# Sparse attention of a two-block layer kernel: scores of large blocks issued a block ahead, small blocks normalised ahead of their neighbour's biases, the last query product counted by halves

## The chip, the cores and the metric

The kernel runs on one core of a Trainium2 chip. The metric is the device time of one execution, in microseconds (us), as the median of several runs.

## The reference, cut to what matters

The whole computes two transformer-like blocks on 1024 tokens. The change touches one part of the second block, `dsa_mixer`, a sparse attention with 4 heads of 64 channels that share one key and one value (MQA). An indexer has scored all admissible keys before; each query keeps its 256 best.

```python
limit = (qpos // CHUNK + 1) * CHUNK            # CHUNK = 64
score = jnp.where(key_pos[None, :] < limit[:, None], score, NEG_BIG)
top_val, top_idx = lax.top_k(score, n_sel)     # n_sel = 256
s = jnp.einsum('bqhd,bqkd->bhqk', qb, k_sel) * (SA_DH ** -0.5)
p = jax.nn.softmax(jnp.where(valid[:, None], s, NEG_BIG), axis=-1)
o = jnp.einsum('bhqk,bqkd->bqhd', p, v_sel)
```

## The kernel before

The kernel is a row of stages; each gives every engine its own program, and semaphores order them. Keys are not gathered. Instead, the stage `sparse_attention` computes dense scores of a block of 128 queries against all keys up to the block's end and adds a mask, zero for kept keys and -1e30 for the others. Block b has (b+1)*128 keys. The blocks are taken in the order 0, 7, 1, 6, 2, 5, 3, 4, so that at place n an even n is a small block (1, 2, 3, 4 tiles of 128 keys) and an odd n a large one (8, 7, 6, 5 tiles).

For each block and head, the work goes around the engines:

- PE, `score_heads` (L3281): for two heads at a time, query times key in two parts (high and low part of the keys), to the PSUM tensors ps0 and ps1, each two banks wide. A head's tensor is free again when DVE has added the bias of the head two before.
- DVE, `bias_scores` (L3216 and L3219): scale, mask, maximum, written to `prob`; then the negated maximum.
- ACT, `exps` (L3158): exponential with the sum. These stand in ACT's program between the evictions of the turns.
- DVE, `normalise` (L3224, L3228): reciprocal, then a multiplication in pieces of two or three key tiles.
- PE, `turn` (L3291): four transposes of one key tile, one per head, to ps2; ACT evicts them (L3173).
- PE, `weigh` (L3300): the product with the values, added up in ps3, one step behind the turns.
- ACT copies the output (L3181, rounded), DVE subtracts for its rest (`rest_o`, L3236).

Two blocks share `prob`: even n at its end, odd n at its start, and no two neighbours overlap. PE's program for block n is: scores of heads 0 and 1 of block n+1, then the turns and weighings of block n, with the scores of heads 2 and 3 of block n+1 behind turn 2 (or the last turn), then the last weighing. DVE's is: biases of heads 0 and 1 of n+1, normalise n, biases of heads 2 and 3 of n+1, rest of the output of n-1. Before a block's biases from n=2 on, DVE waits for the first turn of block n-1, in program terms `pt_ready.at(turns.index((n - 1, 0)))`, which counts all turns before that one.

Before the first block, PE makes the query products, one for each pair of heads (`product`, L322, 48 matmuls each), and between them transposes the keys and values. ACT rounds each to `q_parts` (L3152) and DVE subtracts for the rest (L3199). All scores wait for both pairs of heads with all tokens.

The next stage, `merge`, first issues the gate product; its SP queue waits for the last `rest_o`, then loads a residual of 4 MB, and then the weights that follow.

Of the kernel before, what the change touches and what calls it, by code (L numbers as in the profile page):

```python
# [148 lines left out]
def first_then_second_block(nc, a, out):  # L149
    ctx = ExitStack()  # L150
    with ctx:
# [2929 lines left out]
        def sparse_attention(y_hi_t, y_lo_t, score, kv_t, following):  # L3081
# [7 lines left out]
            with ExitStack() as sc:  # L3089
# [21 lines left out]

                def pieces(n):

                    cuts = [*range(0, order[n], 2), order[n] + 1]
                    return list(zip(cuts, cuts[1:])) if order[n] else [(0, 1)]
# [21 lines left out]
                def _(act):  # L3137
# [8 lines left out]
                    for m in range(2):  # L3146
                        if m == 1:
                            round_chunk(act, 2, 0, 2)
                        act.wait_ge(used.sem, after(used, m, 0, 2))
                        for odd in range(2):  # L3150
                            rows = slice(odd * 64, odd * 64 + 64)
                            last = act.activation(q_parts[rows, 2 * m + odd], ps[m][rows], ACT.Copy)  # L3152
                        last.then_inc(evicted.sem, 1)
# [9 lines left out]
                    for n, b in enumerate(order):  # L3163
                        heads = list(range(H)) if n + 1 < TT else []
                        for j in range(b + 1):
                            if j >= 2 and heads:

                                exps(n + 1, heads.pop(0))
                            x = turns.index((n, j))
                            act.wait_ge(pt_ready.sem, pt_ready.at(x + 1))  # L3170

                            act.wait_ge(o_ready.sem, o_ready.at(x - 1))
                            act.activation(prob_t[:, x % 2], ps[2][:, x % 2 * HALF:x % 2 * HALF + HALF], ACT.Copy)\  # L3173
                               .then_inc(pt_evicted.sem, 1)
# [10 lines left out]
                def _(dve):  # L3185
# [8 lines left out]
                    for m in range(2):  # L3194

                        dve.wait_ge(evicted.sem, evicted.at(m + 1))
                        for odd in range(2):
                            rows, other, h = slice(odd * 64, odd * 64 + 64), slice(64 - odd * 64, P - odd * 64), 2 * m + odd
                            last = dve.tensor_tensor(q_parts[other, h], ps[m][rows], q_parts[rows, h].bitcast(F32), ALU.subtract)  # L3199
                        last.then_inc(aux3.sem, 1)  # L3200
                    dve_steps.wait(dve)
# [6 lines left out]
                    def bias_scores(n, heads):  # L3208
                        b = order[n]

                        if n >= 2:
                            dve.wait_ge(pt_ready.sem, pt_ready.at(turns.index((n - 1, 0))))
# [26 lines left out]

                    bias_scores(0, range(H))  # L3240
                    for n in range(TT):
                        if n + 1 < TT:
                            bias_scores(n + 1, (0, 1))
                        normalise(n)
                        if n + 1 < TT:
                            bias_scores(n + 1, (2, 3))
                        if n >= 1:
                            rest_o(n - 1)
                    rest_o(TT - 1)

                @block.tensor
                def _(pe):
# [13 lines left out]
                    product(pe, (1, 0, 2), wide(ps[1])).then_inc(used.sem, 1)  # L3266
# [37 lines left out]
                    score_heads(0, 2)  # L3304
                    for n in range(TT):
                        if n + 1 < TT:
                            score_heads(n + 1, 0)
                        normed = sum(len(pieces(o)) for o in range(n))
                        for j in range(order[n] + 1):
# [7 lines left out]
                            if j == min(2, order[n]) and n + 1 < TT:  # L3317
                                score_heads(n + 1, 2)
                        weigh(n, order[n])
# [3 lines left out]
            for s, n in ((aux, 2), (aux2, 1), (aux3, 2), (transposed, 1), (tr_evicted, 2), (evicted, 2), (scores, TT * H), (biased, TT * H), (mod_ready, TT * H),  # L3323
# [374 lines left out]
```

## Time and profile before

| | |
|---|---|
| median of 3 runs | 3214.3 us (3212.19 to 3214.42) |
| profiled execution, device time | 3210.17 us |
| its span | 3208.4 us |
| PE busy | 3027.8 us, 94% of the span |
| DVE, ACT, POOL busy | 43%, 30%, 32% |
| chain that ended last, by engine | PE 81%, issue 8%, DVE 6%, POOL 2%, ACT 2% |
| sparse attention, first query product to its last weighing | about 2046 to 2188 us into the span |

Over the whole kernel PE is the engine that sets the time, but the share of the span is an average over stages. In the slice of the page that holds this stage PE's busy digit falls from 9 to 8 and 7 and its clock digit to 8. Views of that stretch say more than the page does: the stretches, the waits and the timeline.

### The profile page before, as it was taken

Reading aid. Unit: us, or ns where it says so; the run is one execution under the profiler, and the core shown is the slowest. Engines: PE = TensorE matmul, PEld = TensorE weight load, DVE = VectorE, ACT = ScalarE, POOL = GpSimd, SP = SyncE. Lnnn points to the kernel's source line nnn. Section 1 sums busy time; section 2 is a strip of 40 time slices with the busy share of each in tenths; the row PEclk is TensorE's granted clock in tenths of the full one; section 3 lists DMA queues with packets and bytes.
Section 4 is the critical chain, followed back from the end, with each engine's and each line's share of the span. In section 5 each row is a group of like instructions: output and inputs, shape, how many; then the busy total and the mean of one; then the engine's idle time right before and its main releaser. Section 6 shows DMA issues by size and latency. Waiting matters only on the chain.

```text
span 3208.4 us, 38389 instructions
## 1 busy us (share of the span) xinstructions
PE 3027.8 (94%) x14387; PEld 2425.3 (76%) x14387; DVE 1367.3 (43%) x2172; ACT 952.0 (30%) x1569; POOL 1015.5 (32%) x801
## 2 busy tenths in 40 slices
PE   7999989999998999999989999978978999999998
PEld 3788768888876877888767888746766888888886
DVE  5344430111011035544387999851275232332325
ACT  3345532122222244231354222242333111111113
POOL 2544322233422345122221333302445332332323
PEclk9999999999999999999999999989988999999999
DMA  5211021111212133111111111102121111111111
GB/s 193 54 37 37 11 85 50 53 46 43 66 51 72 49 92 95 38 27 34 27 47 31 46 49 47 39 1 85 57 66 40 51 47 46 46 52 46 46 52 72
DMA packets 261458, 170.53 MB, mean 53 GB/s; under 512 B 23604, under 2 KB 249452, under 8 KB 260205
## 3 DMA queue, kind: packets, MB, share of 16 engines
q1 hardware_dynamic: 259997, 163.93, 17.1%
q10 hardware_dynamic: 1360, 5.24, 0.4%
q8 instruction: 65, 1.06, 0.1%
q14 instruction: 36, 0.29, 0.0%
HBM read 160.69 MB, written 8.45 MB: 53 GB/s over the span
## 4 chain that ended last, share of the span: by engine, by line
PE 81%; issue 8%; DVE 6%; POOL 2%; ACT 2%; DMA 1%; SPq 0%; POOLq 0%; DVEq 0%; ACTq 0%
PE ps L322 64%; PE ps L3539 2%; PE ps L3538 2%; PE ps L3540 2%; PE ps L2404 2%; DVE score L2985 1%; PE ps L971 1%; PE ps L985 1%; POOL w_lo L306 1%; PE ps L543 1%; DVE ssq L1909 1%; DVE h_lo L1899 1%; PE ps L1490 1%; PE ps L1493 1%; DMA rows<-in_norm_ffn_post 0%
## 5 line engine op out<-in xcount | busy, mean ns | idle before, releaser
L322 PE MATMUL ps<-h_hi,w_hi 128*128 128x512 f32 x2864 | 1142.5, 399 | 53.4 <-POOL w_lo L306 22.7
L322 PE MATMUL ps<-h_lo,w_hi 128*128 128x512 f32 x2864 | 1124.7, 393 | 0.0
L322 PE MATMUL ps<-h_hi,w_lo 128*128 128x512 f32 x2864 | 1123.4, 392 | 0.0
L306 POOL TENSOR_TENSOR w_lo<-raw,w_hi 128x512 fp32r<-128x512 f32 (+2 forms) x556 | 658.9, 1206 | 1394.0 <-ACT w_hi L299 1393.8
L322 PEld LDWEIGHTS ps<-h_hi,w_hi 128*128 128x128 f32 x2864 | 543.7, 190 | 177.1 <-issue 39.8
L322 PEld LDWEIGHTS ps<-h_hi,w_lo 128*128 128x128 f32 x2864 | 543.1, 190 | 116.2
L322 PEld LDWEIGHTS ps<-h_lo,w_hi 128*128 128x128 f32 x2864 | 544.1, 190 | 113.2 <-issue 3.1
L299 ACT ACTIVATE w_hi<-raw 128x512 fp32r<-128x512 f32 (+2 forms) x556 | 288.3, 567 | 891.9 <-PE ps L322 683.3
L3488 DVE TENSOR_TENSOR act<-gate,ps 128x1024 f32<-128x1024 f32 x22 | 26.9, 1221 | 446.1 <-PE ps L322 446.1
L3497 DVE TENSOR_TENSOR acc<-acc,ps 128x1024 f32<-128x1024 f32 x160 | 195.3, 1221 | 28.7 <-PE ps L3540 27.9
L1194 DVE TENSOR_TENSOR part<-sig,ps 128x1024 f32<-128x1024 f32 x40 | 48.6, 1215 | 355.6 <-PE ps L322 274.9
L3073 DVE MATCH_REPLACE8 score<-best,score 128x384 f32<-128x384 f32 (+2 forms) x192 | 165.8, 875 | 0.0
L3074 DVE MAX8 best<-score 128x8 f32<-128x384 f32 (+2 forms) x192 | 155.7, 878 | 1.1
L3539 PE MATMUL ps<-w_lo,act_hi 128*128 128x512 f32 x352 | 140.3, 399 | 0.0
L3538 PE MATMUL ps<-w_hi,act_hi 128*128 128x512 f32 x352 | 139.4, 396 | 0.2 <-POOL w_lo L306 0.2
L3540 PE MATMUL ps<-w_hi,act_lo 128*128 128x512 f32 x352 | 138.1, 392 | 0.0
L3428 POOL TENSOR_TENSOR act_lo<-act,act_hi 128x1024 fp32r<-128x1024 f32 x21 | 50.6, 2408 | 187.2 <-ACT act_hi L3459 187.2
L1152 POOL TENSOR_TENSOR acc<-acc,part 128x1024 f32 x40 | 96.9, 2421 | 0.0
L3459 ACT ACTIVATE act_hi<-act 128x1024 fp32r<-128x1024 f32 x22 | 23.3, 1061 | 217.5 <-DVE act L3488 217.5
L3454 ACT ACTIVATE gate<-ps 128x1024 f32<-128x1024 f32 x22 | 22.6, 1027 | 211.2 <-PE ps L322 211.2
L3538 PEld LDWEIGHTS ps<-w_hi,act_hi 128*128 128x128 f32 x352 | 66.1, 188 | 17.1 <-POOL w_lo L306 0.6
L3540 PEld LDWEIGHTS ps<-w_hi,act_lo 128*128 128x128 f32 x352 | 66.1, 188 | 15.7
(423 smaller groups left out, 3589.2 us busy)
## 6 DMA issues: line engine op xcount, KB each, us to landing
raw<-in_w_in SPq DMA_DIRECT2D x88, 512.0 KB, 4.0
raw<-in_w_ffn_gate_up SPq DMA_DIRECT2D x44, 512.0 KB, 3.8
raw<-in_w_out SPq DMA_DIRECT2D x32, 512.0 KB, 3.7
raw<-in_w_gate SPq DMA_DIRECT2D x32, 512.0 KB, 3.6
raw<-in_w_ffn_down SPq DMA_DIRECT2D x22, 512.0 KB, 3.5
w_ada<-in_w_ada SPq DMA_DIRECT2D x8, 1024.0 KB, 7.8
x_tok<-in_x ACTq DMA_DIRECT2D x4, 1024.0 KB, 14.3
residual_gate<-in_w_ada SPq DMA_DIRECT2D x8, 512.0 KB
```

Of the source, the lines that this page charges most:

```text
L299: act.activation(w_hi[:, s, cut], raw[:, s, cut], ACT.Copy).then_inc(rounded.sem, 1)
L306: pool.tensor_tensor(w_lo[:, s, cut], raw[:, s, cut], w_hi[:, s, cut].bitcast(F32), ALU.subtract).then_inc(split.sem, 1)
L322: last = pe.matmul(dst, w[:, chunk[0] % 2, k], x(k), start=(k == ks[0] and n == 0), stop=(k == ks[-1] and n == 2))
L1152: pool.tensor_tensor(to, to, part[:], ALU.add).then_inc(o_evicted.sem, 1)
L2404: last = pe.matmul(bank[:, cut], keys[:, h % 3, cut], q[:, h % 2, cut] if n == 0 else queries[:, h % 3, cut], start=True, stop=True)
L3073: top_steps.done(dve.match_replace(part(b), best[:, j], part(b), TAKEN) if marking else dve.max(best[:, j], part(b)))
L3074: dve.max(best[:, j], part(b)))
L3428: pool.tensor_tensor(act_lo[:, f % 2], act32[:], act_hi[:, f % 2].bitcast(F32), ALU.subtract)\
L3497: dve.tensor_tensor(acc[:, t], acc[:, t], outs[t][:], ALU.add).then_inc(o_evicted.sem, 1)
L3538: pe.matmul(dst[:, c:c + HALF], act_hi[:, f % 2, tokens], w[0], start=first, stop=False)
L3539: pe.matmul(dst[:, c:c + HALF], act_hi[:, f % 2, tokens], w[1], start=False, stop=False)
L3540: last = pe.matmul(dst[:, c:c + HALF], act_lo[:, f % 2, tokens], w[0], start=False, stop=final)
```

## The change

Three things are changed in `sparse_attention`, and nothing outside of it.

1. The second query product is counted by token halves. Its first 24 matmuls (tokens 0 to 511) increment a semaphore of their own. ACT and DVE take this product in two halves of 512 columns instead of one of 1024, and the first block's scores wait for the first half only. The scores of block n=1 wait for the second half. DVE does that last rest behind the first block's biases.
2. Scores of large blocks are issued a block ahead on PE. Heads 0 and 1 of the large block n+2 stand between the last turn and the last weighing of the large block n, and heads 2 and 3 behind the first turn of the small block between them. For n=1, heads 0 and 1 stand ahead of all turns.
3. On DVE the small block n (even) is normalised ahead of all biases of the large block n+1, and the large block n+1 is normalised ahead of the biases of the small block n+2. The biases now wait for the last turn of block n-2, whose place in `prob` they take. On ACT the exponentials of a large block stand from turn 1 of the small block on, where they stood from turn 2 on.

```diff
                     for m in range(2):
                         if m == 1:
                             round_chunk(act, 2, 0, 2)
-                        act.wait_ge(used.sem, after(used, m, 0, 2))
-                        for odd in range(2):
-                            rows = slice(odd * 64, odd * 64 + 64)
-                            last = act.activation(q_parts[rows, 2 * m + odd], ps[m][rows], ACT.Copy)
-                        last.then_inc(evicted.sem, 1)
+                        for cols in Q_CUTS[m]:
+                            if cols.stop < T:
+                                act.wait_ge(sum_ready.sem, sum_ready.at(1))
+                            else:
+                                act.wait_ge(used.sem, after(used, m, 0, 2))
+                            for odd in range(2):
+                                rows = slice(odd * 64, odd * 64 + 64)
+                                last = act.activation(q_parts[rows, 2 * m + odd, cols], ps[m][rows, cols], ACT.Copy)
+                            last.then_inc(evicted.sem, 1)
...
-                            if j >= 2 and heads:
+                            if (j >= 2 if n % 2 else 1 <= j <= 2) and heads:
 
                                 exps(n + 1, heads.pop(0))
...
                         if n >= 2:
-                            dve.wait_ge(pt_ready.sem, pt_ready.at(turns.index((n - 1, 0))))
+                            dve.wait_ge(pt_ready.sem, pt_ready.at(turns.index((n - 2, order[n - 2])) + 1))
...
+                    rest_q(0, 0)
+                    rest_q(1, 0)
                     bias_scores(0, range(H))
-                    for n in range(TT):
-                        if n + 1 < TT:
-                            bias_scores(n + 1, (0, 1))
+                    rest_q(1, 1)
+                    for n in range(0, TT, 2):
                         normalise(n)
-                        if n + 1 < TT:
-                            bias_scores(n + 1, (2, 3))
+                        bias_scores(n + 1, (0, 1))
+                        bias_scores(n + 1, (2, 3))
                         if n >= 1:
                             rest_o(n - 1)
+                        normalise(n + 1)
+                        if n + 2 < TT:
+                            bias_scores(n + 2, (0, 1))
+                        rest_o(n)
+                        if n + 2 < TT:
+                            bias_scores(n + 2, (2, 3))
                     rest_o(TT - 1)
...
-                    product(pe, (1, 0, 2), wide(ps[1])).then_inc(used.sem, 1)
+                    product(pe, (1, 0, 2), wide(ps[1]), part=(0, 2)).then_inc(sum_ready.sem, 1)
+                    product(pe, (1, 0, 2), wide(ps[1]), part=(1, 2)).then_inc(used.sem, 1)
...
                     score_heads(0, 0)
                     score_heads(0, 2)
+                    pe.wait_ge(aux3.sem, aux3.at(3))
+                    score_heads(1, 0)
                     for n in range(TT):
-                        if n + 1 < TT:
+                        small = n % 2 == 0
+                        if not small and n + 1 < TT:
                             score_heads(n + 1, 0)
...
-                            if j == min(2, order[n]) and n + 1 < TT:
+                            if j == (0 if small else min(2, order[n])) and n + 1 < TT:
                                 score_heads(n + 1, 2)
+                        if not small and n + 2 < TT:
+                            score_heads(n + 2, 0)
                         weigh(n, order[n])
```

## Rows read from the trace of the kernel before

**Rows 1.** Stretches: limits, length, then each engine's busy us and instructions, PE clock.

```profile
2075.40:2096.38 20.98, 11.30 (x35) 8.32 (x34) 12.86 (x37) 11.11 (x22) 0.00 (x0) 0.73 0.00 0
2096.38:2126.16 29.78, 22.98 (x85) 14.33 (x85) 14.79 (x36) 13.63 (x30) 0.00 (x0) 0.84 0.00 1
2126.16:2154.98 28.82, 21.76 (x84) 13.51 (x84) 14.70 (x35) 13.63 (x30) 0.00 (x0) 0.86 0.00 1
2154.98:2181.24 26.26, 21.48 (x81) 13.43 (x81) 13.00 (x30) 13.40 (x30) 0.00 (x0) 0.83 0.00 0
2181.24:2187.99 6.75, 6.50 (x31) 3.79 (x31) 2.46 (x3) 2.88 (x5) 0.00 (x0) 1.00 0.01 2
```

**Rows 2.** Waits of the stage: who waited for whom, us, times, longest.

```profile
DVE prob L3216 <- PE ps L3281: 46.1, 14, 6.6
PEld ps L3291 <- DVE prob L3228: 26.4, 10, 3.8
```

**Rows 3.** Timeline of the start: us, length, engine, line, operation, shapes, idle before.

```profile
2069.51 2.46 DVE L3199 TENSOR_TENSOR q_parts<-ps,q_parts 64x1024 fp32r<-64x1024 f32 x2
...
2075.44 2.05 ACT L3152 ACTIVATE q_parts<-ps 64x1024 fp32r<-64x1024 f32 x2 [5.74 <-PE ps L322]
...
2080.03 0.48 PE L3281 MATMUL ps<-k_hi,q_parts 128*128 128x128 f32 x1 [4.63 <-DVE q_parts L3199]
...
2082.31 0.80 PE L3281 MATMUL ps<-k_hi,q_parts 128*128 128x512 f32 x1
...
2084.43 1.22 DVE L3216 CUSTOM_DVE_ANT_0 prob<-ps,score 128x1024 f32<-128x1024 f32 x1 [1.55 <-PE ps L3281]
...
2092.16 1.22 DVE L3216 CUSTOM_DVE_ANT_0 prob<-ps,score 128x1024 f32<-128x1024 f32 x1 [0.28 <-PE ps L3281]
```

**Rows 4.** Timeline between large block n=1 and large block n=3.

```profile
2105.75 0.19 ACT L3158 ACTIVATION_READ_ACCUMULATOR prob<-prob,stat 128x1 f32 x1
...
2106.82 0.60 PE L3291 MATMUL ps<-ident,prob 128*128 128x128 f32 x4
...
2108.11 0.60 PE L3291 MATMUL ps<-ident,prob 128*128 128x128 f32 x4
...
2109.96 0.80 PE L3281 MATMUL ps<-k_hi,q_parts 128*128 128x512 f32 x1
...
2110.56 0.77 ACT L3181 ACTIVATE yc_hi<-ps 64x256 fp32r<-64x256 f32 x2 [1.22 <-PE ps L3300]
...
2111.50 1.09 DVE L3216 CUSTOM_DVE_ANT_0 prob<-ps,score 128x896 f32<-128x896 f32 x1 [6.59 <-PE ps L3281]
...
2117.40 1.03 ACT L3158 ACTIVATE prob<-prob,stat 128x896 f32<-128x896 f32 x1
```

**Rows 5.** Timeline between large block n=3 and large block n=5.

```profile
2135.61 0.60 PE L3291 MATMUL ps<-ident,prob 128*128 128x128 f32 x4
...
2141.20 1.76 DVE L3228 TENSOR_TENSOR prob<-prob,stat 128x1536 f32<-128x1536 f32 x1
```

**Rows 6.** Timeline between large block n=5 and large block n=7.

```profile
2164.11 0.71 ACT L3158 ACTIVATE prob<-prob,stat 128x512 f32<-128x512 f32 x1
...
2169.53 2.36 DVE L3228 TENSOR_TENSOR prob<-prob,stat 128x1024 f32<-128x1024 f32 x2
...
2181.24 1.09 PE L3291 MATMUL ps<-ident,prob 128*128 128x128 f32 x8 [1.96 <-DVE prob L3228]
```

**Rows 7.** Two short stretches with PE's clock, and the loads around one turn.

```profile
2100.00:2102.50 2.50, 2.50 (x8) 1.57 (x7) 0.00 (x0) 1.08 (x3) 0.00 (x0) 0.54 0.00 0
2105.00:2107.50 2.50, 2.50 (x13) 1.54 (x12) 0.00 (x0) 1.59 (x5) 0.00 (x0) 1.00 0.00 0
...
2099.20 0.23 PEld L3291 LDWEIGHTS ps<-ident,prob 128*128 128x128 f32 x1 [0.52 <-issue]
...
2101.76 0.34 PEld L3281 LDWEIGHTS ps<-k_hi,q_parts 128*128 128x128 f32 x1 [0.52 <-issue]
```

**Rows 8.** Timeline of the next stage: the rounding that waits for gate weights.

```profile
2204.64 1.15 ACT L299 ACTIVATE w_hi<-raw 128x512 fp32r<-128x512 f32 x2 [13.46 <-DMA raw<-in_w_gate]
```

More of the change, by code:

```diff
@@ L3110, in out_of @@
                     return ps[3][half * 64:half * 64 + 64, c:c + 2 * P].rearrange("p (t c) -> p t c", c=P)
+                Q_CUTS = ((slice(0, T),), (slice(0, HALF), slice(HALF, T)))
                 def pieces(n):
@@ L3193, in _, with rest_q @@
                         dve_steps.done(dve.tensor_scalar(x, x, TAKEN, NEG, ALU.not_equal, ALU.mult))
-                    for m in range(2):
-                        dve.wait_ge(evicted.sem, evicted.at(m + 1))
+                    dve_steps.wait(dve)
+                    def rest_q(m, c):
+                        cols = Q_CUTS[m][c]
+                        dve.wait_ge(evicted.sem, evicted.at(m + c + 1))
                         for odd in range(2):
                             rows, other, h = slice(odd * 64, odd * 64 + 64), slice(64 - odd * 64, P - odd * 64), 2 * m + odd
-                            last = dve.tensor_tensor(q_parts[other, h], ps[m][rows], q_parts[rows, h].bitcast(F32), ALU.subtract)
+                            last = dve.tensor_tensor(q_parts[other, h, cols], ps[m][rows, cols], q_parts[rows, h, cols].bitcast(F32),
+                                                     ALU.subtract)
                         last.then_inc(aux3.sem, 1)
-                    dve_steps.wait(dve)
                     def mask(b):
@@ L3322, in sparse_attention @@
             X = len(turns)
-            for s, n in ((aux, 2), (aux2, 1), (aux3, 2), (transposed, 1), (tr_evicted, 2), (evicted, 2), (scores, TT * H), (biased, TT * H), (mod_ready, TT * H),
+            for s, n in ((aux, 2), (aux2, 1), (aux3, 3), (sum_ready, 1), (transposed, 1), (tr_evicted, 2), (evicted, 3), (scores, TT * H), (biased, TT * H), (mod_ready, TT * H),
                          (exped, TT * H), (probs, sum(len(pieces(n)) for n in range(TT))), (pt_ready, X), (pt_evicted, X), (o_ready, X), (o_evicted, TT), (y_hi, TT)):
```

## The prediction

> **What bounds the kernel now.** The change lies in one stage, sparse attention, so I read the views of that stage only. First the stretches [rows 1]: I cut the stage where the first transposes (L3291) of the large blocks begin, which gives a start, three cycles of one large and one small block, and an end. The five add up to 112.6 us, of which TensorE is busy 84.0 and VectorE 57.8. Neither is full, so this is a chain of handovers. Then the waits of the stage [rows 2]: DVE waits 46.1 us for scores and the transposes wait 26.4 us for normalised probabilities. They are two halves of one round trip: PE makes scores, DVE adds the bias (L3216), ACT takes the exponential (L3158), DVE normalises (L3228), PE transposes. Between one large block and the next large block this round trip begins only when the large block is wholly transposed and weighed: the last turn of block 1 is at 2108.11, the first score of block 3 at 2109.96, its first transposes only at 2126.16 [rows 1, 4]. Below, n counts places in the order (even n small, odd n large), and T1, T3, T5, T7 are the starts of the first turns of the large blocks: 2096.38, 2126.16, 2154.98, 2181.24 [rows 1].
>
> Behind the stage, merge loads its residual only when the last rest of the output is done; the gate weights queued behind it are rounded at 2204.64 [rows 8]. That wait counts from the end of this stage, so it moves with it and gives nothing back. I price the changed stage alone.
>
> **Start (product to T1).** The eviction of the last query product is cut in two, so that its first half (ACT) and that half's rest (DVE) run beside the second half of the product. The nearest rows are two 64x1024 pieces, 2.05 us on ACT and 2.46 on DVE, and two 64x256 pieces, 0.77 on ACT [rows 3, 4]. Two 64x512 pieces should then take about 1.2 us on ACT and about 1.4 on DVE (estimates between these rows; bounds 0.77 and 2.05, and for DVE half of 2.46 and 2.46). DVE is free of the first query rest at 2069.51+2.46=2071.97, and ends the first half of the second by 2073.4, hidden by the product, which runs to 2075.4. So the small first block's scores start at 2075.4 in place of 2080.03 [rows 3]. From its first score to the first large scores it takes 2.28 us now (2080.03 to 2082.31), all its biases included but the last, so those end at about 2077.65. The added wait, on the last half's rest, holds up the first large scores: DVE does it behind the four biases, 2077.65+1.4. So they start at 2079.05, not at 2082.31. ACT has the second half done at 2076.65 and the short exponentials behind it are off this path. From there the path is: first bias of block 1 2.12 us later (2082.31 to 2084.43 [rows 3]), 2081.2; second bias to about 2083.8. The transposes of block 0 now stand behind these scores on PE (2082.1 to 2082.6), then come the third head's scores: 2.0 us from issue to bias, 2084.6. The fourth needs the second bias; it is issued at 2084.3 and its bias starts 1.95 later, 2086.25. From the fourth bias (2092.16 [rows 3]) to T1 it is 4.22 us now, so T1 = 2090.5. Gain **5.9 us**.
>
> **Cycle 1 to 3.** The first two heads' scores of block 3 move ahead of the last weighing of block 1. The last turn is at T1+11.73 (2108.11), and the previous weighing is issued 0.87 later, so the scores start at T1+12.6. From score to first bias 1.54 (2109.96 to 2111.50), each further bias 1.20: biases at 14.1 and 15.3, done at 16.5. The moved scores put the last weighing 2.05 us back, to 14.65; its eviction follows 1.16 later, ACT 15.8 to 16.6 [rows 4]. Normalising the small block 2 is done by T1+11.0, beside the turns of block 1 (its exponentials end at 2105.94, T1+9.6 [rows 4], as now), so it leaves this path; its cover is the 3.6 us before the biases. PE then does turn(2,0) to 15.8, scores of the third head to 17.0, of the fourth to 17.9, turn(2,1) to 18.6. ACT is in order: eviction of turn(2,0) 16.6 to 17.1, exponential of head 0 to 18.2, then it waits for turn(2,1), 18.6 to 19.2. This is the new bottleneck, since the exponential of head 1, ready at 16.5, is queued behind it. Three exponentials at 1.02 with the read of the sum [rows 4] end at 22.3, DVE's normalisation takes 0.2 and 1.3 for its first piece: T3 = T1+23.8 against 29.8. Gain **6.0 us**. The two small biases that now stand behind the normalisation of block 1 (4.6 us of DVE) delay the first small exponential to T1+4.1, and the third turn's eviction behind it is at T1+4.8 anyway: nothing, as long as normalising stays under that.
>
> **Cycle 3 to 5**, the same way. Last turn at T3+9.45 (2135.61 [rows 5]), scores 10.4, first bias 11.8, second done 13.9. Weighing 12.2, eviction to 14.1, turn(4,0) to 13.4, scores of the last two heads to 15.2, turn(4,1) 15.2 to 15.8. ACT: turn 14.7, exponential 15.5, turn 16.5, exponential 17.3, turn(4,2) 18.0, two exponentials to 19.8; T5 = T3+21.3 against 28.8. Gain **7.5 us**, of which 2.0 is the one piece of 1536 (1.76 us [rows 5]) that no longer stands between the biases and the turns.
>
> **Cycle 5 to 7.** Scores at T5+10.2 would give the bias at 11.5, but the last small exponential ends at T5+9.8 (2164.11 and 0.71) and normalising block 6 takes 0.2+2.36 [rows 6], so DVE is free only at 12.4: here the cover is gone and costs 0.9 us. Biases at 12.4 and 13.3, scores of the last heads to 15.0; ACT then threads three evictions and two exponentials up to turn(6,3), 18.9, and two more to 20.7. T7 = T5+22.2 against 26.3. Gain **4.1 us**. The end behind T7 (6.75 us [rows 1]) issues the same work in the same order: nothing.
>
> **The sum** is 5.9+6.0+7.5+4.1 = 23.5 us. The profiled execution took 3210.2 us (span 3208.4); less 23.5 it is 3186.7. The median of the runs shown is 4.1 above it, 3214.3, so I expect 3190.8, rounded 3191. The path above counts few of the handovers between engines that are not in a measured interval; each of the four parts has some three, and 0.1 to 0.5 us each on twelve makes 1 to 6 us too little. On the other side the 10 us of stretches that wait at the lower clock could shrink. The estimated halves of the eviction can move the start by -0.8 or +1.9.
>
> **Clock, a rule weighed.** Rows first: at 2100 to 2102.5 the granted clock is 0.54, which is the 1.2 GHz level nearly throughout, and one turn with its weighing takes 2.56 us (2099.20 to 2101.76); at 2105 to 2107.5 it is 1.00, the 2.4 GHz level, and a turn takes 1.29 (2106.82 to 2108.11) [rows 4, 7]. The low stretches follow idle PE. I kept the low stretch behind each T. The Trainium skill, "TensorE: Matmul & The Clock Gate", Part 4 (PE-mode transpose), says that the full clock does not engage for transposes. This trace doesn't bear that out: the stretch at 1.00 is turns and weighings alone.
>
> **Rivals.**
> (a) *Clock stays high.* PE's idle time before T5 and T7 falls to about 2 us, and before T7 of the old kernel a stop of 1.96 us [rows 6] was followed by clock 1.00 [rows 1]. If the three turns behind T1, T3 and T5 run high, they save up to 3 x 1.27 = 3.8 us each, less 0 to 2 us where DVE's pieces of 1.2 us hold them: 4 to 8 us, **3185**. Against: it needs every stop to be short. Chance 0.15.
> (b) *ACT's order is the bound.* The exponentials put between a small block's turns wait for biases that themselves wait for PE, and the turns behind them wait for ACT. If in each cycle the large exponentials start only behind the last small turn's eviction, one to two more of them (1.0 us each) and a round of waits are added, some 3 us a cycle: 23.5-9 = 14.5, **3200**. For: ACT is already the last to be ready in all three cycles. Chance 0.13.
> (c) *The gain is given back.* Were the next stage's weights bound to something before this stage's end, the 23.5 us would turn into a longer wait at 2204.64: **3213**. Against: the residual load is issued only at that end. Chance 0.02.
> (d) *Slower.* Scores leave the places where they broke up the turns, and the clock falls for the whole stage. Of 36 turns about 13 are at the low level now; the other 23 would cost 1.27 more each, 29 us, and about 60 of the 96 score matmuls 0.2 more, up to 8 us in the open parts only, say 1: 30-23.5 = 6.5, **3221**. It decides from 19 turns on that change level. The rule of the page above would be its ground. Against: PE has less idle time per cycle afterwards. Chance 0.03.
>
> **How the numbers follow.** The forecast, 3187 to 3197 with its own size errors, has 0.67. With (a) 0.15, (b) 0.13, (c) 0.02, (d) 0.03 it makes 1. Range: from 3183 (rival a with the start's lower bound) to 3202 (rival b, with 2 us for the medians). A measurement of this kernel tells 0.2%, 6.4 us, from no change: faster than 3207.9 is all of forecast, (a) and (b), 0.95, of which I leave 0.02 to mixtures that end inside; within 0.2% is 0.04; slower 0.03.
>
> **What would show it.** In the changed profile: first score of block 0 about 0.1 us behind the product (if not, the half isn't free early); first large score some 3.7 us later; T1 15 us behind the product's end in place of 21; score matmuls between last turn and last weighing of each large block; one idle stretch of PE a cycle, not two, of 2 to 3 us; cycles of 24, 21 and 22 us. The large exponentials should be what DVE's normalisation waits for last. The prediction is wrong if PE waits for ACT's evictions within the large block's turns, if DVE's wait for scores doesn't fall well under 46 us, or if the granted clock of the cycles drops below the present 0.83 to 0.86.

## The result, and the profile after

The changed kernel takes 3184.9 us (median of four runs, 3182.65 to 3189.05) where the kernel before takes 3213.3 (four runs). The ratio is 0.9919, 95% interval 0.9907 to 0.993: some 26 us less. The forecast was 3191 with a range of 3183 to 3202, so direction and range held, and the gain was forecast a little small: the median lies below the 3187 to 3197 that the forecast gave its own size errors, and on the 3185 of rival (a).

The two profiled executions can't be subtracted as a whole. In the one of after, this stage begins 4.1 us later, though nothing ahead of it changed: the transposes of the values (L3263 before, L3278 after) start at 2063.40 and 2067.51. Over all profiles below that start lies between 2063.3 and 2068.2. So every stage time here is taken from the first of these transposes to the first gate matmul of the next stage, and cut at T1, T3, T5 and T7 as in the prediction. Stretches of the kernel before, the first from the transposes on (columns: limits, length, busy us and instructions of PE, PE's loads, DVE, ACT, POOL, then PE's granted clock as a share of 2.4 GHz, DMA share, GB/s):

```profile
2063.40:2096.38 32.98, 23.30 (x92) 18.08 (x90) 19.14 (x46) 16.19 (x29) 2.69 (x3) 0.83 0.01 4
...
sum 124.59, PE 96.02 PEld 63.13 DVE 64.08 ACT 59.73 POOL 2.69; mean PE 19.20 PEld 12.63 DVE 12.82 ACT 11.95 POOL 0.54
```

The same stretches of the changed kernel:

```profile
2067.51:2094.79 27.28, 22.05 (x93) 17.44 (x91) 18.40 (x42) 16.37 (x31) 2.69 (x3) 0.87 0.02 5
2094.79:2117.27 22.48, 19.52 (x85) 12.65 (x85) 14.61 (x36) 13.31 (x30) 0.00 (x0) 0.92 0.00 1
2117.27:2137.07 19.80, 18.30 (x85) 11.52 (x85) 14.63 (x35) 13.08 (x30) 0.00 (x0) 1.00 0.00 1
2137.07:2156.92 19.85, 17.61 (x81) 10.88 (x81) 14.60 (x36) 13.19 (x30) 0.00 (x0) 1.00 0.00 0
2156.92:2164.93 8.01, 8.01 (x30) 4.68 (x31) 2.46 (x3) 2.99 (x5) 0.00 (x0) 0.79 0.01 2
```

Beside [rows 1]: the stage went from 124.59 to 97.42 us, 27.2 less. The start gave 5.7, the cycles 7.3, 9.0 and 6.4, and the end took 1.3 back. DVE does the same work (64.1 and 64.7 us busy); PE's busy time fell by 10.5 us with the same 14387 matmuls in the kernel, while its granted clock rose: 0.84, 0.86, 0.83 in the cycles before, 0.92, 1.00, 1.00 after.

The waits of the stage after (who waited for whom, us, times, longest):

```profile
...
DVE stat L3232 <- ACT prob L3164: 13.6, 8, 3.4
...
PEld ps L3307 <- DVE prob L3236: 10.7, 5, 3.0
DVE prob L3224 <- PE ps L3297: 9.6, 9, 3.1
```

Against [rows 2], DVE's wait for scores fell from 46.1 to 9.6 us, and the transposes' wait for DVE from 26.4 to 10.7, 10 times to 5. The new wait is the first line: DVE, before it normalises, waits 13.6 us for ACT's exponentials.

The place between block 1 and block 3, to be read against [rows 4] (timeline: start, length, engine, line, operation):

```profile
2105.57 0.60 PE L3307 MATMUL ps<-ident,prob 128*128 128x128 f32 x4
...
2106.47 0.80 PE L3297 MATMUL ps<-k_hi,q_parts 128*128 128x512 f32 x1
...
2107.99 1.09 DVE L3224 CUSTOM_DVE_ANT_0 prob<-ps,score 128x896 f32<-128x896 f32 x1 [3.12 <-PE ps L3297]
...
2109.56 0.77 ACT L3187 ACTIVATE yc_hi<-ps 64x256 fp32r<-64x256 f32 x2 [2.75 <-PE ps L3316]
...
2110.84 1.04 ACT L3164 ACTIVATE prob<-prob,stat 128x896 f32<-128x896 f32 x1
...
2112.57 1.03 ACT L3164 ACTIVATE prob<-prob,stat 128x896 f32<-128x896 f32 x1
...
2115.64 0.76 ACT L3187 ACTIVATE yc_hi<-ps 64x256 fp32r<-64x256 f32 x2
2115.77 0.18 DVE L3232 RECIPROCAL stat<-stat 128x4 f32<-128x4 f32 x1 [1.60 <-ACT prob L3164]
...
2117.27 1.09 PE L3307 MATMUL ps<-ident,prob 128*128 128x128 f32 x8 [2.71 <-DVE prob L3236]
```

The last turn is at T1+10.8, the scores at +11.7, the first bias 1.52 later, ACT busy with hardly a gap from 2109.56 to 2115.74, where the last exponential ends, normalisation, T3. This is the order of steps that the prediction wrote down; its times were up to 1.4 us later (last exponential at T1+22.3, measured +20.95). The last turns of blocks 3 and 5, against T3 (2117.27) and T5 (2137.07), and the last turn of block 5 before, against its T5 (2154.98):

```profile
2125.68 0.60 PE L3307 MATMUL ps<-ident,prob 128*128 128x128 f32 x4
2144.19 0.60 PE L3307 MATMUL ps<-ident,prob 128*128 128x128 f32 x4
```

```profile
2164.28 0.60 PE L3291 MATMUL ps<-ident,prob 128*128 128x128 f32 x4
```

### The profile page after: what moved, and what is told of

Its sections match the earlier page's. It is cut to its first block, busy times and chain, and to the rows that moved or that the text cites. A ratio compares the mean times of both kernels' runs of the same rounds, so it can differ in the third digit from the quotient of the medians.

```text
span 3185.0 us, 38394 instructions
## 1 busy us (share of the span) xinstructions
PE 3020.8 (95%) x14387; PEld 2422.2 (76%) x14387; DVE 1368.4 (43%) x2174; ACT 951.5 (30%) x1571; POOL 1016.9 (32%) x801
## 4 chain that ended last, share of the span: by engine, by line
PE 82%; issue 7%; DVE 6%; POOL 2%; ACT 2%; DMA 1%; SPq 0%; POOLq 0%; DVEq 0%; ACTq 0%
PE ps L322 64%; PE ps L3560 2%; PE ps L3559 2%; PE ps L3561 2%; PE ps L2404 2%; DVE score L2985 1%; PE ps L971 1%; PE ps L985 1%; POOL w_lo L306 1%; PE ps L543 1%; DVE ssq L1909 1%; DVE h_lo L1899 1%; PE ps L1490 1%; PE ps L1493 1%; DMA rows<-in_norm_ffn_post 0%
```

## The experiments

All times of a stage part are taken from each kernel's own profile. The columns are start (to T1), the three cycles, the end, and their sum; the ratio to before is that of the timed runs.

| kernel | start | 1 to 3 | 3 to 5 | 5 to 7 | end | sum | ratio |
|---|---|---|---|---|---|---|---|
| before | 33.0 | 29.8 | 28.8 | 26.3 | 6.8 | 124.6 | 1 |
| changed | 27.3 | 22.5 | 19.8 | 19.9 | 8.0 | 97.4 | 0.9919 |
| changed, again | 26.1 | 23.6 | 20.6 | 19.8 | 8.0 | 98.1 | 0.9915 |
| halves alone (a1) | 29.5 | 29.9 | 28.8 | 26.3 | 6.8 | 121.2 | 0.9985 |
| changed without halves (a2) | 29.5 | 23.5 | 20.6 | 19.8 | 8.0 | 101.5 | 0.9925 |
| DVE's order alone (a3) | 29.5 | 24.2 | 21.4 | 21.7 | 8.0 | 104.7 | 0.9934 |
| the same, again (d1) | 30.6 | 23.1 | 22.9 | 20.0 | 6.7 | 103.3 | 0.9941 |
| PE's order alone (a4) | 33.0 | 26.2 | 26.7 | 24.4 | 6.8 | 116.9 | 0.9977 |
| DVE's and ACT's order (e1) | 30.2 | 22.9 | 22.8 | 20.0 | 6.8 | 102.7 | 0.9939 |
| changed, ACT's order old (b1) | 26.0 | 24.5 | 22.7 | 19.8 | 8.0 | 101.1 | 0.9927 |
| changed, extra matmuls (b2) | 26.0 | 21.6 | 20.2 | 19.8 | 6.8 | 94.4 | 0.9902 |
| changed, ACT relieved (c1) | 27.2 | 21.9 | 19.4 | 17.7 | 7.0 | 93.2 | 0.9906 |
| relieved, extra matmuls (c2) | 25.4 | 21.1 | 19.4 | 17.8 | 7.0 | 90.6 | 0.9895 |

A cycle has two parts that behave differently. From T to the large block's last turn PE works through turns, and profiles of one kernel differ there by up to 1.7 us, with the clock. From the last turn to the next T (the tail of the cycle, from here on) the engines wait for each other, and there two profiles of one kernel agree within 0.03 us. So the tails tell more of an edit of the orders than whole cycles do:

| kernel | T1 to last turn, tail | T3 to last turn, tail | T5 to last turn, tail | sum of the tails |
|---|---|---|---|---|
| before | 11.7, 18.05 | 9.5, 19.38 | 9.3, 16.96 | 54.4 |
| changed | 10.8, 11.70 | 8.4, 11.39 | 7.1, 12.73 | 35.8 |
| changed, again | 11.9, 11.71 | 9.3, 11.39 | 7.1, 12.70 | 35.8 |
| a1 | 11.8, 18.06 | 9.5, 19.36 | 9.3, 16.97 | 54.4 |
| a2 | 11.8, 11.72 | 9.2, 11.40 | 7.1, 12.72 | 35.8 |
| a3 | 11.8, 12.43 | 8.4, 13.02 | 8.8, 12.87 | 38.3 |
| d1 | 10.7, 12.44 | 9.9, 13.01 | 7.1, 12.87 | 38.3 |
| a4 | 9.3, 16.88 | 9.3, 17.36 | 8.4, 15.98 | 50.2 |
| e1 | 10.5, 12.43 | 9.7, 13.12 | 7.1, 12.86 | 38.4 |
| b1 | 11.8, 12.72 | 10.4, 12.31 | 7.1, 12.70 | 37.7 |
| b2 | 9.9, 11.69 | 8.4, 11.83 | 7.1, 12.70 | 36.2 |
| c1 | 10.7, 11.13 | 8.4, 10.94 | 7.1, 10.59 | 32.7 |
| c2 | 9.9, 11.14 | 8.4, 10.94 | 7.2, 10.60 | 32.7 |

**Halves alone.** The query product in halves as in the changed kernel, all loops of DVE, PE and ACT as before. DVE's loop, against the changed kernel:

```diff
                     rest_q(1, 1)
-                    for n in range(0, TT, 2):
+                    for n in range(TT):
+                        if n + 1 < TT:
+                            bias_scores(n + 1, (0, 1))
                         normalise(n)
-                        bias_scores(n + 1, (0, 1))
-                        bias_scores(n + 1, (2, 3))
+                        if n + 1 < TT:
+                            bias_scores(n + 1, (2, 3))
...
```

> Part 1 of the change alone (query product counted and taken in halves), all orders as before. Theory S (the steps of the prediction, but followed with the old DVE order): the first large scores start 3.3 us earlier (2082.31 to 2079.05 in the old trace's time), but the small block 0 is still normalised behind two large biases, so the rest of the start keeps its length and the cycles are unchanged: 3.3 us faster than before, ratio 0.999. Rival (as the prediction booked it): the whole gain of the start, 5.9 us, belongs to this part: ratio 0.998, and the first turns of block 1 come 5.7 us sooner behind the product than before.

Measured: ratio 0.9985 (0.9976 to 0.9994), 4.8 us by the ratio; in the profile the start is 3.5 us shorter and every cycle is what it was, within 0.07 us. By the profile theory S holds. The interval of the timed runs, 1.9 to 7.7 us, doesn't tell 3.3 from 5.9. The timeline shows why the start doesn't give more:

```profile
2078.73 0.80 PE L3293 MATMUL ps<-k_hi,q_parts 128*128 128x512 f32 x1 [2.00 <-DVE q_parts L3207]
...
2082.28 1.23 DVE L3224 CUSTOM_DVE_ANT_0 prob<-ps,score 128x1024 f32<-128x1024 f32 x1
...
2083.82 0.69 DVE L3236 TENSOR_TENSOR prob<-prob,stat 128x512 f32<-128x512 f32 x1
2084.57 0.66 PE L3303 MATMUL ps<-ident,prob 128*128 128x128 f32 x4 [2.33 <-DVE prob L3236]
```

The large scores start sooner, but block 0 is normalised only behind the second large bias, and PE, with the next large scores queued behind block 0's transposes, stands 2.33 us. That stop is DVE's order, which this kernel has unchanged.

**Without halves.** One cut of all tokens for the second product, one rest, no third wait.

```diff
-                Q_CUTS = ((slice(0, T),), (slice(0, HALF), slice(HALF, T)))
+                Q_CUTS = ((slice(0, T),), (slice(0, T),))
...
                     bias_scores(0, range(H))
-                    rest_q(1, 1)
...
-                    pe.wait_ge(aux3.sem, aux3.at(3))
                     score_heads(1, 0)
```

> The changed kernel with part 1 taken back (second query product waited for whole, one rest of 1024 columns ahead of the first biases), orders as changed. Theory S: 3.3 us slower than the changed kernel, about 24 us faster than before, ratio 0.9925. Rival: 5.7 us slower than the changed kernel, about 21.5 faster than before, ratio 0.993, if the start's gain is all of this part.

Measured: 0.9925 (0.9912 to 0.9939); the stage is 4.0 and 3.4 us longer than in the two profiles of the changed kernel, the start 2.2 and 3.4 longer. The cycles equal those of the changed kernel's second profile within 0.03 us. That is nearer to theory S, though it doesn't pin the size: the start of a2 has the clock at 0.87, as the first profile of the changed kernel has (2.2 us between them) and unlike the second (0.92, 3.4 us). The halves are worth 2.2 to 3.4 us here and 3.5 alone, not 5.7.

**DVE's order alone, PE's order alone.** Each on the kernel before. DVE's order alone (a3):

```diff
-                    for n in range(TT):
-                        if n + 1 < TT:
-                            bias_scores(n + 1, (0, 1))
-                        normalise(n)
-                        if n + 1 < TT:
-                            bias_scores(n + 1, (2, 3))
...
+                    for n in range(0, TT, 2):
+                        normalise(n)
+                        bias_scores(n + 1, (0, 1))
+                        bias_scores(n + 1, (2, 3))
...
```

PE's order alone (a4):

```diff
                     score_heads(0, 2)
+                    score_heads(1, 0)
                     for n in range(TT):
-                        if n + 1 < TT:
+                        small = n % 2 == 0
+                        if not small and n + 1 < TT:
                             score_heads(n + 1, 0)
...
-                            if j == min(2, order[n]) and n + 1 < TT:
+                            if j == (0 if small else min(2, order[n])) and n + 1 < TT:
                                 score_heads(n + 1, 2)
+                        if not small and n + 2 < TT:
+                            score_heads(n + 2, 0)
```

> The kernel before with only DVE's order changed (small block normalised ahead of the large biases, large block ahead of the small biases); PE, ACT and the query product as before. Theory D: taking the small normalisation and the small biases out of the round trip is what carries the cycles; the scores come 1 us later than in the changed kernel but the exponentials are ready in about the same time. Start 2.6 us, cycles 6.4, 6 and 4 us: about 19 us faster than before, ratio 0.994. Rival P (the scores issued a block ahead carry the cycles): at most 10 us faster, ratio 0.997 or more, with the small block's normalisation merely moved into a wait for scores.

> The kernel before with only PE's order changed (scores of large blocks a block ahead, third and fourth head behind the first small turn); DVE, ACT and the query product as before. Theory D: normalising the small block still stands between the large biases and the small turns, so each cycle gains only the 1 us of the hidden weighing and some 2 us of earlier third and fourth scores: about 8 us faster than before, ratio 0.9975. Rival P: 15 us or more faster, ratio 0.995 or less.

Measured: DVE's order alone 0.9934 (0.992 to 0.9947), 21 us; PE's alone 0.9977 (0.9968 to 0.9986), 7.4 us. In the profiles the stage falls by 19.9 and 7.7 us. Theory D holds and rival P falls. What the one repairs and the other doesn't is in the waits. DVE's order alone:

```profile
DVE prob L3216 <- PE ps L3285: 17.1, 9, 4.1
PEld ps L3295 <- DVE prob L3228: 11.1, 5, 2.8
```

PE's order alone:

```profile
DVE prob L3216 <- PE ps L3281: 34.3, 16, 5.6
PEld ps L3291 <- DVE prob L3228: 26.3, 11, 4.1
```

With DVE's order the transposes wait 5 times, only at the large blocks: PE's stops ahead of the small blocks 2, 4 and 6 (3.20, 3.59 and 2.81 us before) are gone, and those ahead of T3 and T5 fell from 3.12 and 3.28 to 2.21 and 1.99. With PE's order alone the transposes wait as long as before, 26.3 us, since every small block still stands behind two large biases. DVE's order was changed at two places, ahead of the large biases and ahead of the small ones; no run takes the two apart.

**The same kernel again.**

> The kernel of a3_dve_order_only once more, beside a fast variant on the same chip: it tells how far two profiles of one kernel differ in this stage. Theory K: the stage's parts differ by up to 1.3 us each, with the clock in which the first scores and turns fall, and the sum by under 1.5 us. Rival: parts and sum repeat within 0.3 us, so that differences of that size between kernels are due to their edits.

Measured: the parts differ from the first profile by 1.1, 1.1, 1.5, 1.7 and 1.3 us, the sum by 1.5. The rival, that they repeat within 0.3 us, falls; one single part of one profile tells nothing under 2 us. In all five parts the longer one has the lower clock, and the tails agree within 0.01 us. T7 and the next 2.5 us in the two, with PE's stop ahead of it 1.97 us long in both:

```profile
2162.50 1.90 PE L3295 MATMUL ps<-ident,prob 128*128 128x128 f32 x8 [1.97 <-DVE prob L3228]
...
2162.50:2165.00 2.50, 2.50 (x9) 2.00 (x10) 2.46 (x3) 1.17 (x2) 0.00 (x0) 0.52 0.00 0
```

```profile
2161.26 1.09 PE L3295 MATMUL ps<-ident,prob 128*128 128x128 f32 x8 [1.97 <-DVE prob L3228]
...
2161.26:2163.76 2.50, 2.25 (x12) 1.48 (x13) 2.46 (x3) 1.09 (x2) 0.00 (x0) 1.00 0.00 0
```

**ACT's order taken back.**

```diff
-                            if (j >= 2 if n % 2 else 1 <= j <= 2) and heads:
+                            if j >= 2 and heads:
```

> The changed kernel with ACT's order taken back: the large exponentials stand from turn 2 of the small block on, as before, in place of turn 1. Theory A (ACT's in-order queue is the bound of the new cycles): the exponentials end 1.0, 1.2 and 0.5 us later in the three cycles, 2.7 us slower than the changed kernel, about 24.5 us faster than before, ratio 0.9923. Rival: ACT is not what ends last, since DVE's biases and PE's turns set the same time; no difference from the changed kernel (0.9915 to 0.992), the cycles agree with its 22.5, 19.8 and 19.9 us within 0.3.

Measured: 0.9927 (0.9914 to 0.9941) against 0.9919 and 0.9915 for the changed kernel. The three cycles come to 67.1 us against 62.1 and 64.0. With the second of these, whose clock rows at T1 and T3 are alike (0.92, 0.86 and 0.92, 0.85), the cycles are 1.0, 2.1 and 0.0 us longer, 3.1 in sum, where theory A had 1.0, 1.2 and 0.5. But the part of 3 to 5 holds a low clock too (0.88 for 0.93). By the tails, the old order costs 1.0, 0.9 and 0.0 us: 1.9, where theory A had 2.7. Theory A holds in the first two cycles; in the last the change of ACT's order gave nothing. By the timed intervals alone the two kernels are not told apart.

**DVE's and ACT's order, PE's as before.** The same line of ACT, here as in the changed kernel, on top of a3.

> The kernel of a3_dve_order_only with ACT's order changed as well (large exponentials from turn 1 of the small block on); PE's order and the query product as before. So it is the changed kernel without the scores a block ahead and without the halves. Theory J (the two need each other): with the scores late, the biases of the third and fourth head end last, about 20.8 us behind T1, and earlier places for the exponentials give at most 0.5 us a cycle; the three cycles stay at 66 to 67 us in sum as in the two profiles of a3 (67.3 and 66.0), ratio 0.994. Rival: ACT's order alone brings the 4 to 5 us by which the changed kernel's cycles (62.1) are shorter, the cycles come to 62 to 63 us, ratio 0.9925, and the scores a block ahead bring nothing.

Measured: 0.9939 (0.9926 to 0.9953). The cycles take 65.7 us, against 67.3 and 66.0 with DVE's order alone. Theory J holds: the tails are 38.4 us in sum, against 38.3 twice, so ACT's new order alone gives nothing. And b1, with PE's order and without ACT's, has cycles of 67.1 and tails of 37.7, 0.6 less. Both together bring the tails to 35.8, 2.5 less: most of what earlier scores could give is used up waiting in ACT's queue unless ACT's program asks for them sooner.

**The changed kernel again.** The same kernel, profiled and timed a second time.

> The changed kernel once more, on the same chip. It tells how far its own profiles differ. Theory K (the clock behind a stop of 1 to 3 us falls in some executions and not in others): start, cycles and end differ from the first profile (27.3, 22.5, 19.8, 19.9, 8.0) by 1 to 1.5 us each where the clock row differs, the sum of the stage within 2 us of 97.4, ratio to before 0.9905 to 0.993. Rival: the parts repeat within 0.3 us, the end of 8.0 us included, and the low clock behind T7 belongs to the change.

Measured: 0.9915 (0.9901 to 0.9928), stage 98.1 us. Start and first two cycles differ by 1.2, 1.1 and 0.8 us, as theory K had it (beside 0.92 and 1.00 in the first profile, the clock of the first two cycles is 0.86 and 0.93), and the tails within 0.03; but the end is 8.0 us in both, and T7 is at the low clock in both:

```profile
2089.82:2113.38 23.56, 20.84 (x85) 13.53 (x85) 14.62 (x36) 13.52 (x30) 0.00 (x0) 0.86 0.00 1
2113.38:2134.02 20.64, 19.40 (x84) 12.58 (x85) 14.62 (x35) 13.27 (x30) 0.00 (x0) 0.93 0.00 1
...
2153.84:2161.86 8.02, 8.02 (x31) 4.72 (x31) 2.46 (x3) 2.98 (x5) 0.00 (x0) 0.79 0.01 2
```

Of the other profiles with a start of T7 behind a stop of 1.96 or 1.97 us, a2, a3 and b1 have 8.0, before, a1, a4, d1 and e1 6.7 to 6.8. So it isn't the length of the stop, and it isn't the kernel alone, since a3 and d1 are one. What decides it stays open.

**Extra matmuls ahead of the large blocks.** They write what the turn behind them overwrites, and let PE work where it would stop.

```diff
                                 normed += 1
+                                if j == 0 and not small:
+                                    x = turns.index((n, 0))
+                                    pe.wait_ge(pt_evicted.sem, pt_evicted.at(x - 1))
+                                    c = x % 2 * HALF
+                                    for _ in range(8):
+                                        pe.matmul(ps[2][:, c:c + HALF], q_parts[:, 0, 0:P], k_hi[:, 0:HALF], start=True, stop=True)
                                 pe.wait_ge(probs.sem, probs.at(normed))
```

> The changed kernel with 8 extra matmuls of 512 columns on PE ahead of its wait for each large block's first normalised piece; they write the half of ps2 that the turn behind them overwrites, so nothing that is computed changes. Theory K (the low clock behind PE's stops is a cost of its own): the turns behind T1 and T7 run at the full clock; last turn of block 1 at T1+9.7 in place of +10.8, next stage at T7+6.8 in place of +8.0, together about 2 us faster than the changed kernel, less at most 0.6 us where the wait was only 1.25 us long. Rival: the clock doesn't follow this, or the turns are held by other engines: no gain, and up to 2 us slower, as the extra matmuls outlast the waits.

Measured: 0.9902 (0.9887 to 0.9918), which overlaps with the intervals of the changed kernel; stage 94.4 us, 3.1 and 3.7 less than its two profiles. Of the 3.1, 1.3 lie in the start, ahead of the first extra matmul, where the second profile of the changed kernel is as short; so 1.8 and 3.7 us are left for the extra matmuls. The clock behind T1, in the changed kernel and then with the extra matmuls:

```profile
2095.00:2097.50 2.50, 2.25 (x10) 1.37 (x9) 2.50 (x3) 1.08 (x2) 0.00 (x0) 0.67 0.03 7
2097.50:2100.00 2.50, 2.50 (x8) 1.47 (x7) 2.38 (x9) 1.30 (x4) 0.00 (x0) 0.65 0.00 0
```

```profile
2094.50:2097.00 2.50, 2.25 (x15) 1.49 (x14) 2.50 (x3) 1.09 (x2) 0.00 (x0) 1.00 0.00 0
2097.00:2099.50 2.50, 2.48 (x13) 1.38 (x12) 2.39 (x10) 1.33 (x4) 0.00 (x0) 1.00 0.00 0
```

The last turn of block 1 is at T1+9.91 (2104.16 behind 2094.25) in place of 10.78 and 11.85, that of block 3 at T3+8.40 in place of 8.41 and 9.25, and the end takes 6.75 in place of 8.01: near the two sizes that theory K named (9.7 and 6.8). The 3 to 5 cycle is 0.4 longer, where eight matmuls outlast a wait of 1.25 us. The low clock behind a stop is thus a cost of its own, 0.9 to 1.9 us a time here. The Trainium skill, "TensorE: Matmul & The Clock Gate", section "HAM oscillation — how this bites in real kernels", describes kernels whose TensorE falls back to the low clock at each wait, and advises a loop order that keeps it busy; these rows agree, with waits for another engine in place of its waits for loads.

**ACT relieved.** DVE makes the rounded copy of blocks 1, 3 and 5 (`Y_DVE`), and a small block's turns have more exponentials between them.

```diff
-                            if (j >= 2 if n % 2 else 1 <= j <= 2) and heads:
-
-                                exps(n + 1, heads.pop(0))
+                            for _ in range(1 if n % 2 and j >= 2 else 0 if n % 2 or j < 1 else 2 if j == 1 else 1):
+                                if heads:
+                                    exps(n + 1, heads.pop(0))
...
+                        if n in Y_DVE:
+                            continue
                         act.wait_ge(o_ready.sem, o_ready.at(turns.index((n, b)) + 1))
...
+                        if n in Y_DVE:
+                            dve.wait_ge(o_ready.sem, o_ready.at(turns.index((n, b)) + 1))
+                            for half in range(2):
+                                rows = slice(half * 64, half * 64 + 64)
+                                dve_steps.done(dve.tensor_scalar(y_hi_t[rows, :, b * P:b * P + P], out_of(n, half), 1.0, None, ALU.mult))
+                            dve_steps.wait(dve)
...
```

> The changed kernel with work taken off ACT: the rounded copy of the output of blocks 1, 3 and 5 is made by DVE ahead of its rest, and two large exponentials stand behind the first turn of a small block, one behind each further turn. Theory A (ACT's in-order queue is the bound of the new cycles): the last exponential ends 0.6, 0.2 and 1.8 us sooner in the three cycles, 2.6 us faster than the changed kernel, ratio to before about 0.991. Rival: ACT isn't the bound, or DVE's added 0.85 us of copying takes its place: no gain, or up to 1 us slower in the cycle from 1 to 3.

Measured: 0.9906 (0.9891 to 0.9921), stage 93.2 us. The cycles are 0.6, 0.5 and 2.1 us shorter than in the first profile of the changed kernel, for 0.6, 0.2 and 1.8 expected, and the tails are shorter by the same amounts than in both; the end at 7.0 us came at the full clock. DVE's wait for ACT is nearly halved:

```profile
DVE stat L3235 <- ACT prob L3165: 7.6, 7, 1.8
```

Theory A holds, in the last cycle clearly. The edit does two things, and no run tells the moved copy from the moved exponentials. The timed interval overlaps with those of the changed kernel.

**Both.** The relieved kernel, with 7 extra matmuls ahead of the first large scores, 8 ahead of T1 and 6 ahead of T3:

```diff
+                    for _ in range(7):
+                        pe.matmul(ps[2][:, 0:HALF], q_parts[:, 0, 0:P], k_hi[:, 0:HALF], start=True, stop=True)
                     pe.wait_ge(aux3.sem, aux3.at(3))
                     score_heads(1, 0)
...
+                                if n in {1: 8, 3: 6} and j == 0:
...
+                                    for _ in range({1: 8, 3: 6}[n]):
...
```

> The kernel of c1_act_relief with extra matmuls of 512 columns where PE still waits: 7 ahead of the first large scores, 8 ahead of T1, 6 ahead of T3, into parts of ps2 that are written again before they are read. Theory K (the clock behind a stop is a cost of its own, start included): the first large scores run at the full clock, T1 comes 1.9 us sooner behind the product than in c1 (25.3 in place of 27.2 us behind the transposes of the values), the turns of block 1 take 1 us less; together 2.5 to 3 us faster than c1, ratio to before 0.990. Rival: start and turns are then held by DVE's 1.2 us pieces and biases, and the clock gives less than 1 us, within the scatter of the runs.

Measured: 3179.0 us, 0.9895 (0.9879 to 0.9912); stage 90.6 us, 2.6 less than c1; start 25.4, where theory K had 25.3. The tails are those of c1 within 0.01 us; what is gained is clock. Of the 2.6 us, 1.8 lie in the start, and there profiles of the same orders without extra matmuls lie between 26.0 and 27.3; against the shortest of them the start gains 0.6. The start's stretch has the clock at 1.00:

```profile
2068.17:2093.55 25.38, 23.25 (x107) 17.80 (x106) 18.21 (x42) 16.60 (x31) 2.66 (x3) 1.00 0.02 5
```

It is the fastest kernel here by its median and by its stage. Its interval overlaps with that of the changed kernel, so that it is faster than the changed kernel rests on the parts of the profiles.

## Why the prediction was right, and where its terms were off

The sum was 23.5 us; the stage gave 27.2 in the first profile and 26.5 in the second, and the timed ratio 26. Term by term, with the changed kernel's two profiles:

- **Start, 5.9: measured 5.7 and 6.9.** The size was right, and so were the steps: the first small scores, the first large scores, the four large biases and T1 all came within 0.6 us of their forecast places. The owner was not. The prediction gave it all to the halves. Halves alone give 3.5, and DVE's order alone 3.5 and 2.4, since it takes the stop of 2.32 us ahead of block 0's turn away. The prediction said that block 0's transposes "now" stand behind the first large scores; they did before, too. Another part of the diff was nothing: the new wait of the biases names the last turn of block n-2, which is the same count as the old one.
- **Cycle 1 to 3, 6.0: measured 7.3 and 6.2.** From the last turn to T3 it took 11.7 us in both, for 12.1 worked out. What is left is the turns of block 1, last turn at T1+10.8 and +11.9 for 11.7.
- **Cycle 3 to 5, 7.5: measured 9.0 and 8.2.** From the last turn on 11.4 in both, for 11.9; the last turn at T3+8.4 and +9.3 for 9.45.
- **Cycle 5 to 7, 4.1: measured 6.4 and 6.4.** From the last turn on 12.7 in both, for 12.9; the last turn at T5+7.1 in both for 9.3.
- **End, nothing: measured -1.3 and -1.3.** The work is the same; T7 fell into the low clock. Other kernels with the same end have 6.7.

So the step that was mis-sized is the one on the clock: "I kept the low stretch behind each T". The handovers were worked out 0.2 to 0.5 us too long each, 1.0 in sum, and the turns of the three large blocks took 4.2 us less than booked in the first profile and 2.3 in the second. This was rival (a), with 4 to 8 us for it; it came in part, 4.2 or 2.3 us less the 1.3 of the end. Its 1.27 us for each of nine turns was too much as well: at the full clock throughout (b2) the last turns are at +9.9, +8.4 and +7.1, only 5.1 us in all ahead of the booked 11.7, 9.45 and 9.3. b2 shows for blocks 1 and 3 that the clock, and not the order, is what those turns hang on. That the median, 3184.9, falls on rival (a)'s 3185 is in part luck: of the 6.1 us between it and the forecast the stage gave 3.0 to 3.7, the median before came 1.0 lower with its fourth run, and the rest is scatter of the medians. The estimated eviction of half a product was good: 0.59 us a piece on ACT and 0.69 on DVE in the changed profile, for 0.6 and 0.7.

Rival (b), ACT's order as the bound, was right as a mechanism and wrong as a loss: ACT is what ends last (13.6 us of waits), and c1 takes 3.2 us out there, but the chain with ACT in it was already the one that the sum went by. Rivals (c) and (d) fell. The rounding of the gate weights ([rows 8]) starts at 2181.59 where this was 2204.64, 16.7 us behind the stage's end in both, and the clock of the cycles rose.

What the prediction didn't have is which edit carries how much. By the runs, DVE's order alone brings 20 to 21 of the 27 us of stage, PE's order alone 7.7. Laid on DVE's order, by the tails, ACT's brings nothing, PE's 0.6 us and both together 2.5; the cycles as a whole show 2 to 5 us for the two, the clock included. The halves bring 2.2 to 3.5.

## What to carry to other kernels

Where two blocks of unequal size go around the same engines, ask first what stands between the small block's last input and its use in the engine that serves both: here it was half of the other block's work on DVE, and moving that was worth more than issuing TensorE's work earlier. An earlier producer pays only if each in-order queue behind it asks for its output earlier too; change the queue of the next engine with it, or the gain is waited away there. And price stops of TensorE twice, once for their length and once for the low clock behind them.

## What the runs showed of the hardware that was not expected

- A stop of PE of the same length is followed by the low clock in one execution and not in another: 1.97 us ahead of T7 in two profiles of one kernel (a3, d1), then 0.52 and 1.00 in the 2.5 us behind it, 8.0 and 6.7 us to the end of the stage. In the changed kernel a stop of 2.71 us ahead of T3 was followed by no low clock in one profile and by one in the other (eight transposes in 1.09 and in 1.97 us).
- Transposes run at the full clock when it is granted: eight of them took 1.09 us at T3 of the changed kernel's first profile and 1.97 in its second, at the low clock. A stretch of turns and weighings alone even brings the clock back, as the changed kernel shows behind T7. The page that the prediction quoted, the Trainium skill, "TensorE: Matmul & The Clock Gate", Part 4, has it otherwise for transposes; what transposes with nothing between them would do behind a stop, no run here shows.

```profile
2158.50:2161.00 2.50, 2.50 (x8) 1.36 (x8) 0.88 (x3) 0.60 (x1) 0.00 (x0) 0.56 0.04 7
2161.00:2163.50 2.50, 2.50 (x13) 1.45 (x13) 0.00 (x0) 1.20 (x2) 0.00 (x0) 1.00 0.00 0
```

- Extra matmuls that compute nothing made the stage shorter: 32 of them took 1.8 to 3.7 us out of that of the changed kernel, 21 took up to 2.6 out of that of the relieved one. In the timed runs the intervals still overlap.
